# A three-block network on one core: the quarter boundaries and the tail of block 3 in another order

## The chip, the core and the metric

The kernel runs on one core of one Trainium2 chip. TensorE (PE) multiplies, VectorE (DVE), ScalarE (ACT) and GpSimd (POOL) do the rest, and SyncE (SP) issues most transfers; each engine runs its own list of instructions in order and waits on semaphores. The metric is the time of one whole execution on the device, in microseconds, as the median of several runs.

## What is computed

Three blocks follow each other on 2048 rows of 1024 float32 numbers; the change is in the third. Its reference, cut to what matters:

```python
h = einsum('btd,de->bte', x, w_in) + b_in            # 36 column tiles of 128
q_a, k_a, v_a, g_a, q_h, z_fwd, z_bwd, i_h, g_h = split(h, ...)
o_a = neighbourhood_attention(q_a, k_a, v_a, rpb) * silu(g_a)
logf_f, k_f = hgrn2_forget(z_fwd, ...)
logf_b, k_b = hgrn2_forget(z_bwd, ...)
o_fwd = hgrn2_chunk_scan(q_h, k_f, i_h, logf_f)      # S_t = f_t S_{t-1} + k_t v_t
o_bwd = flip(hgrn2_chunk_scan(flip(q_h), flip(k_b), flip(i_h), flip(logf_b)))
o_h = o_fwd + o_bwd
o_h = o_h * rsqrt(mean(square(o_h), -1) + RMS_EPS) * hg_norm_gain * silu(g_h)
y = einsum('bte,ed->btd', concatenate([o_a, o_h], -1), w_out) + b_out
r = DEEPNORM_ALPHA * x + y
out = (r - mean(r)) * rsqrt(var(r) + LN_EPS) * ln_gain + ln_bias
```

## The kernel before, in words

Every float32 factor of the large products is split into a high part and the remainder, and each product is three matmuls (high x high, high x low, low x high).

**Quarters.** Block 3 works on four quarters of 512 rows. In each, 36 column tiles of the input projection run (24 matmuls of 512 columns each, L3804 to L3806, or the same work by rows, L3814 to L3816). Between them stand pieces of attention and of the recurrence. At the start of a quarter x is needed transposed and split: `turn_x` i is, for row tile i of 16, eight transposes into two PSUM banks (x2_turn, L3045), a copy by ScalarE that makes the high part (x2_high, L3055), and a subtraction by VectorE for the low part (x2_low, L3062). Two SBUF buffers hold row tiles, so tile i + 2 can be loaded only after tile i is transposed, and the two PSUM banks are shared with the projection.

**Recurrence.** 64 units (quarter, head, direction, half). For each, `el` is 15 VectorE and 11 ScalarE instructions that make the scaled factors, `prod` (products, L3823 to L3845) sums small blocks into one PSUM bank, opened and closed by matmuls of zeros (L3823, L3834), `state` and `out` (outputs, closed by L3877) follow one and two slots later. The backward direction has no running state yet: its states come last, in 16 chain units n = 0 to 15, four heads of the last quarter first.

**Tail.** Chain unit n loads four 128x512 pieces (`ch_ld`: query, key-value, output so far, gate), VectorE makes four states (chain_state, L3748, L3751), TensorE multiplies them with the query (L3948), VectorE adds (`ch_o`, L3686), ScalarE squares (`sq`), TensorE sums over channels (`fin`, L3957), ScalarE makes the root as logarithm and exponential (`fin_root`, L3450, L3453), VectorE scales and gates (`fin2`, L3691, L3693), and SyncE stores the result to y_tiles in HBM (L3273). The output projection takes 16 row tiles from the last row to the first. Each loads its y tile (`y_ld`, L3296), splits it (`y_split`: ACT L3458, DVE L3701), and multiplies it in two halves of 24 matmuls of 512 columns (`o`, L254 to L256) with w_out, which was loaded (`wo`, L3251), and split by ScalarE (L3438) and GpSimd (L3781, `wo_split`). x is loaded (`x_ld`), GpSimd adds the bias to it (L3787), which VectorE has scaled once (`o_scale`, L3696), VectorE adds the product (`o_sum`, L3707), takes statistics of both halves (`o_end`, L3713), and normalises (L3718, L3724) with a root from ScalarE (`o_root`, L3463, L3465).

**Order.** One list, L.order, made by b3_order, holds all these steps; each engine walks through it and emits its part of each step. A step is placed before or behind a slot (`before`, `after`); slots 0 to 143 are the projection tiles, 36 to a quarter, slots behind that the tail. Inside a slot a rank decides.

## Time and profile before

| | us |
|---|---|
| median of 3 runs (lowest, highest) | 4450.73 (4446.66, 4456.67) |
| the profiled execution | 4447.12 |
| its span | 4445.2 |

Stretches of the span (us from its start), TensorE's busy time in them, its granted clock as a share of 2.4 GHz, and the busy share of the 16 DMA engines:

| stretch | what runs | PE busy | clock | DMA |
|---|---|---|---|---|
| 2900 to 3080 | most of quarter 0 | 151.1 of 180 | 0.85 to 1.00 | 0.71 to 0.86 |
| 3120 to 3160 | first boundary | 23.4 of 40 | 0.85, 0.72 | 0.91, 0.47 |
| 3160 to 3180 | quarter 1 | 20.0 of 20 | 1.00 | 0.45 |
| 3440 to 3480 | second boundary | 31.0 of 40 | 1.00, 0.74 | 0.62, 0.39 |
| 3760 to 3800 | third boundary | 31.0 of 40 | 1.00, 0.74 | 0.58, 0.42 |
| 4160 to 4240 | end of the recurrence, chain units | 33.9 of 80 | 0.59 to 0.74 | 0.44 to 1.01 |
| 4260 to 4320 | chain units and out projection | 60.0 of 60 | 1.00 | 0.33 to 0.68 |

How to read it: busy time of TensorE is no measure of speed, since its matmuls overlap; its idle time is what a better order can win. A wait has a releaser, the last event it waited for, and a wait that ends costs only if nothing else ends later.

### The profile page before, as it was taken

How to read it: one execution, taken by the hardware profiler on the slowest of the kernel's cores; microseconds unless marked ns; L12 is line 12 of the kernel's file. 1: busy time of each engine (PE TensorE's matmuls, PEld its weight loads, DVE VectorE, ACT ScalarE, POOL GpSimd, SP SyncE). 2: the span in 40 equal slices, each digit the busy share in tenths (PEclk: the TensorE clock that was granted, in tenths of full speed). 3: DMA queues.
4: the chain of work that ended last, by engine and by line, in shares of the span. 5: the costliest groups of instructions: out<-in, count | busy, mean ns of one | idle time of the engine just before them, and what ended most of it. 6: DMA issues, size and time to landing. Idle time of an engine off the chain costs nothing.

```text
span 4445.2 us, 62175 instructions
## 1 busy us (share of the span) xinstructions
PE 4200.8 (95%) x24346; PEld 3427.1 (77%) x24346; DVE 2689.6 (61%) x4238; ACT 1799.4 (40%) x3434; POOL 664.2 (15%) x308
## 2 busy tenths in 40 slices
PE   6999999999999999999999989988899999999689
PEld 5888888889888877788777768867787787777467
DVE  6788888872666643045377767555456546466466
ACT  5111111111566631122466556445445446355553
POOL 2111111110333321111012212322000000000111
PEclk9999999999999999999999999999999999999799
DMA  5111111122544431111488872578666466556553
GB/s 184 43 53 53 52 53 53 53 72 93 192 128 128 124 116 48 64 58 73 174 265 294 271 273 105 192 226 282 218 208 199 159 209 197 182 182 199 187 184 131
DMA packets 515499, 663.94 MB, mean 149 GB/s; under 512 B 60476, under 2 KB 407424, under 8 KB 491786
## 3 DMA queue, kind: packets, MB, share of 16 engines
q1 hardware_dynamic: 466778, 577.13, 40.0%
q10 hardware_dynamic: 48432, 82.85, 5.0%
q8 instruction: 195, 3.19, 0.3%
q14 instruction: 94, 0.77, 0.1%
HBM read 442.24 MB, written 217.65 MB: 148 GB/s over the span
## 4 chain that ended last, share of the span: by engine, by line
PE 78%; DMA 6%; DVE 6%; ACT 4%; SPq 3%; issue 2%; POOL 1%; ACTq 0%; DVEq 0%; POOLq 0%
PE ps L229 11%; PE ps L230 11%; PE ps L231 11%; PE ps L255 3%; PE ps L254 3%; PE ps L256 3%; PE ps L3804 3%; DMA w_split_tiles<-w 3%; PE ps L3805 3%; PE ps L3806 3%; PE ps L3924 2%; PE ps L242 1%; PE ps L243 1%; PE ps L244 1%; PE ps L3893 1%
## 5 line engine op out<-in xcount | busy, mean ns | idle before, releaser
L229 PE MATMUL ps<-hh,wsplit 128*128 128x512 f32 x2048 | 819.9, 400 | 5.5 <-DVE hl L953 3.7
L230 PE MATMUL ps<-hl,wsplit 128*128 128x512 f32 x2048 | 808.6, 395 | 0.0
L231 PE MATMUL ps<-hh,wsplit 128*128 128x512 f32 x2048 | 807.8, 394 | 0.0
L982 DVE SCALAR_TENSOR_TENSOR conv_acc<-conv_in,pcol,conv_acc 128x1024 f32<-128x1024 f32 x480 | 687.4, 1432 | 14.8
L229 PEld LDWEIGHTS ps<-hh,wsplit 128*128 128x128 f32 x2048 | 386.5, 189 | 98.2 <-issue 7.8
L230 PEld LDWEIGHTS ps<-hl,wsplit 128*128 128x128 f32 x2048 | 390.1, 190 | 91.6 <-issue 4.3
L231 PEld LDWEIGHTS ps<-hh,wsplit 128*128 128x128 f32 x2048 | 388.6, 190 | 88.9
L221 POOL TENSOR_TENSOR wsplit<-wraw,wsplit 128x1024 fp32r<-128x1024 f32 x72 | 203.8, 2841 | 1327.6 <-ACT wsplit L216 1327.6
L3804 PE MATMUL ps<-h_hi,w 128*128 128x512 f32 x896 | 377.5, 421 | 18.5 <-DVE b_ost L3527 6.1
L3805 PE MATMUL ps<-h_lo,w 128*128 128x512 f32 x896 | 356.9, 398 | 0.0
L3806 PE MATMUL ps<-h_hi,w 128*128 128x512 f32 x896 | 355.9, 397 | 0.0
L733 ACT ACTIVATE b_sig<-ps 128x512 f32<-128x512 f32 x64 | 38.3, 600 | 502.5 <-PE ps L231 502.0
L3804 PEld LDWEIGHTS ps<-h_hi,w 128*128 128x128 f32 x896 | 171.4, 191 | 62.8 <-DVE b_ost L3527 6.7
L3805 PEld LDWEIGHTS ps<-h_lo,w 128*128 128x128 f32 x896 | 172.8, 193 | 41.0 <-issue 0.3
L3806 PEld LDWEIGHTS ps<-h_hi,w 128*128 128x128 f32 x896 | 171.8, 192 | 39.7
L254 PE MATMUL ps<-wo,o_yh 128*128 128x512 f32 x448 | 177.4, 396 | 3.1 <-DVE o_yl L1108 3.1
L3781 POOL TENSOR_TENSOR wo<-wo_raw,wo 128x1024 fp32r<-128x1024 f32 x8 | 18.5, 2344 | 1076.2 <-ACT wo L3438 1076.2
L256 PE MATMUL ps<-wo,o_yl 128*128 128x512 f32 x448 | 176.6, 394 | 0.0
L255 PE MATMUL ps<-wo,o_yh 128*128 128x512 f32 x448 | 176.5, 394 | 0.0
L3814 PE MATMUL ps<-w,h_hi 128*128 128x256 f32 x512 | 153.9, 301 | 12.0 <-POOL w L3018 10.0
L242 PE MATMUL ps<-wsplit,hh 128*128 128x256 f32 x512 | 147.6, 288 | 5.0 <-POOL wsplit L221 5.0
L3815 PE MATMUL ps<-w,h_hi 128*128 128x256 f32 x512 | 148.3, 290 | 0.0
(427 smaller groups left out, 8765.0 us busy)
## 6 DMA issues: line engine op xcount, KB each, us to landing
w<-w_split_tiles SPq DMA_DIRECT2D x108, 1024.0 KB, 5.4
wraw<-in_w_in SPq DMA_DIRECT2D x72, 512.0 KB, 3.9
w_split_tiles<-w SPq DMA_DIRECT2D x36, 1024.0 KB, 6.9
sh<-hy_ak ACTq DMA_DIRECT2D x48, 512.0 KB, 4.0
g_tiles<-b_ost SPq DMA_DIRECT2D x80, 256.0 KB, 5.6
w_raw<-in_w_in SPq DMA_DIRECT2D x36, 512.0 KB, 4.7
wo_raw<-in_w_out SPq DMA_DIRECT2D x32, 512.0 KB, 6.3
sh<-hy_ad ACTq DMA_DIRECT2D x32, 512.0 KB, 8.7
```

Of the source, the lines that this page charges most:

```text
L221: e.tensor_tensor(self.H[:, n % self.ring, 1024:2048], self.raw[:, n % 2, :], self.H[:, n % self.ring, 0:1024], ALU.subtract).then_inc(*c. ...
L229: e.matmul(p[:, :], wh, c.HH[tb][:, k, :], start=k == 0, stop=False)
L230: e.matmul(p[:, :], wh, c.HL[tb][:, k, :], start=False, stop=False)
L231: t = e.matmul(p[:, :], wl, c.HH[tb][:, k, :], start=False, stop=k == 7)
L242: e.matmul(out, hh, wh, start=k == 0, stop=False)
L254: e.matmul(p[:, :], yh(k), wh, start=k == 0, stop=False)
L255: e.matmul(p[:, :], yh(k), wl, start=False, stop=False)
L256: t = e.matmul(p[:, :], yl(k), wh, start=False, stop=k == KT - 1)
L982: e.scalar_tensor_tensor(v, a[:, h * 1024 + j:(h + 1) * 1024 + j], c.convw(j, ch), v, ALU.mult, ALU.add) \
L3804: e.matmul(p[:, :], wh, L.HH[:, k, :], start=k == 0, stop=False)
L3805: e.matmul(p[:, :], wh, L.HL[:, k, :], start=False, stop=False)
L3806: t = e.matmul(p[:, :], wl, L.HH[:, k, :], start=False, stop=k == 7)
```

## The change

**Boundaries.** The first two row tiles of a quarter are loaded four slots sooner. `turn_x` i, i + 1, i + 2 and i + 3 no longer come in two pairs, but with the steps of the slot between them, and all four ahead of the element step `el`. The load of tile i + 2 is issued by ScalarE behind its copy of tile i, not by SyncE.

**Zeros.** L3834 and L3877 are gone; the last real matmul closes the sum.

**Tail.** w_out tiles 0 to 3 and chain unit 0 are loaded within the last slots of the projection. Units 1 to 4, the attention half of y tile 0, w_out 4 to 7, and units 5 to 9 follow behind the recurrence, then the three constants. The first four units' root and scaling are done in one group, and fin2 writes the 128 columns of row tile 15 straight into the buffer of y tile 0. The out projection begins in slot 158 instead of 160. Its statistics are taken per half behind each sum, and its root is now an addition and a reciprocal by VectorE and one square root by ScalarE.

```diff
-    L.cb, L.fb = Banks(c, c.P[5:6]), Banks(c, c.P[6:8])
+    L.cb, L.fb = Banks(c, c.P[5:6]), Banks(c, c.P[6:8] + c.P[2:4])
...
     for k in range(8):
-        after(148 if k < 4 else 150, "wo", k)
+        after((143, 144, 141, 142)[k] if k < 4 else c0 + 1, "wo", k)
     for k in range(0, 8, 4):
-        after(151 if k < 4 else 153, "wo_split", k)
-    c0 = 149
+        after(c0 if k < 4 else c0 + 7, "wo_split", k)
     for n in range(16):
         s = c0 + n
-        after(c0 if n < 4 else c0 + 4 if n < 10 else c0 + 8 if n < 12 else c0 + 11 if n < 14 else c0 + 13, "ch_ld", n)
+        after(c0 - 5 if n < 1 else c0 if n < 5 else c0 + 2 if n < 10 else c0 + 9 if n < 12 else c0 + 11 if n < 14 else c0 + 13, "ch_ld", n)
         after(s + 1, "chain", n)
         after(s + 2, "ch_o", n)
         after(s + 3, "sq", n)
         after(s + 3, "fin", n)
-        if n % 2:
-            after(s + 4, "fin_root", n)
-            after(s + 5, "fin2", n)
-    o0 = c0 + 11
-    after(c0 + 1, "o_const")
-    after(o0 - 4, "o_scale")
+        if n == 3:
+            after(s + 3, "fin_root", 0, 1, 2, 3)
+            after(s + 3, "fin2", 0, 1, 2, 3)
+        elif n % 2 and n > 3:
+            after(s + 4, "fin_root", n - 1, n)
+            after(s + 5, "fin2", n - 1, n)
+    o0 = c0 + 9
+    after(c0 + 5, "o_const")
+    after(o0 - 1, "o_scale")
     for i in range(16):
         s = o0 + 2 * i
-        after(s - 2, "y_ld", i)
+        after(s - 2 if i else c0 + 1, "y_ld", i)
...
-        if s in L.begin and s:
-            L.order += [("turn_x", 4 * (s // 36) + j) for j in range(2, 4)]
         if s < 144:
             L.order += slots[s]
-            if s + 6 in L.begin:
-                L.order += [("row_ld", 4 * ((s + 6) // 36) + j) for j in range(2)]
+            if s + 10 in L.begin:
+                L.order += [("row_ld", 4 * ((s + 10) // 36) + j) for j in range(2)]
             L.order += [("put", u) for u in (slots[s - 1] if s else [])]
         if s == 144:
             L.order += [("put", u) for u in slots[143]]
+        late = sorted(post.get(s, []), key=lambda x: 30 if x[0] == "el" else rank.get(x[0], 20))
         if s + 1 in L.begin:
-            L.order += [("turn_x", 4 * ((s + 1) // 36) + j) for j in range(2)]
-        L.order += sorted(post.get(s, []), key=lambda x: 30 if x[0] == "el" else rank.get(x[0], 20))
+            i = 4 * ((s + 1) // 36)
+            early = [x for x in late if x[0] in ("ld", "w_st", "out", "state")]
+            mid = [x for x in late if x not in early and x[0] != "el"]
+            L.order += [("turn_x", i)] + early + [("turn_x", i + 1)] + mid + [("turn_x", i + 2), ("turn_x", i + 3)] + [x for x in late if x[0] == "el"]
+        else:
+            L.order += late
...
-        elif k == "turn_x" and s[1] >= 4 and s[1] % 4 < 2:
-            row_ld(s[1] + 2)
...
-            if s[1] == 0:
+            k = s[1]
+            if k < 4:
+                for n in range(140, 144):
+                    if w3_slot(n) == k:
+                        e.wait_ge(*L.done[L.last_unit[n]])
+                    if n % 4 == k:
+                        e.wait_ge(*L.w_ld[k][n])
+            else:
                 e.wait_ge(*L.done[L.last_unit[143]])
-            if s[1] >= 4:
-                e.wait_ge(*L.wo_hi[s[1] - 4])
+                e.wait_ge(*L.wo_hi[k - 4])
...
+            if n < 4:
+                e.wait_ge(*L.o_st[n % 2][12 + n])
             if n == 0:
+                for u in (first_of(3, 0) + 2, first_of(3, 0) + 3):
+                    e.wait_ge(*L.qe_st[u % 4][u])
+                    e.wait_ge(*L.kv_st[u % 2][u])
+                stored((3, "rg", 0))
+            elif n == 1:
                 e.wait_ge(*L.r_pe[63, "out", 1])
-                for q in L.qe_st + L.kv_st + L.o_st + L.ost_st:
+                for q in L.qe_st + L.kv_st + L.ost_st:
...
+                m = 384 if n < 4 else 512
                 e.wait_ge(*L.fin_d[n, 1])
                 if n >= 4:
                     e.wait_ge(*L.ry_st[n % 4][n - 4])
-                e.dma_start(c.Y[4 + hd][:, 512 * tb:512 * tb + 512], L.CB[chain_buffer(n)][:, 2, :]).then_inc(*L.ry_st[n % 4].up(n))
+                e.dma_start(c.Y[4 + hd][:, 512 * tb:512 * tb + m], L.CB[chain_buffer(n)][:, 2, 0:m]).then_inc(*L.ry_st[n % 4].up(n))
...
+            if i == 0:
+                for w in att_needed(L, it):
+                    e.wait_ge(*L.y_st[w % 2][w])
+                e.dma_start(L.Y2raw[b][:, 1024:1536].rearrange("p (k t) -> p k t", k=4), c.Y[0:4, :, it * 128:(it + 1) * 128].rearrange("k p t -> p k t")) \
+                    .then_inc(*L.y_ld[b].up(i))
+                continue
...
+            elif i:
+                e.wait_ge(*L.ry_st[3][3])
...
             x2_high(e, c, i)
+            if i % 4 < 2:
+                e.wait_ge(*L.tr[i, 1])
+                x2_load(e, c, i + 2)
...
-            e.wait_ge(*L.o_dve["mv", i])
-            e.activation(v, L.sto[:, i % 2, 13:14], ACT.Ln, bias=L.eps5).then_inc(*L.o_act.up((i, 0)))
-            e.wait_ge(*L.o_act[i, 0])
-            e.activation(v, v, ACT.Exp, scale=-0.5).then_inc(*L.o_act.up((i, 1)))
+            e.wait_ge(*L.o_dve["inv", i])
+            e.activation(v, v, ACT.Sqrt).then_inc(*L.o_act.up((i, 1)))
...
+                if n < 4:
+                    to = L.Y2raw[0][:, 1536 + 128 * hd:1664 + 128 * hd]
+                    e.tensor_tensor(to, yo[:, 384:512], ga[:, 384:512], ALU.mult).then_inc(*L.fin_d.up((n, "y")))
+                e.tensor_tensor(yo[:, 0:m], yo[:, 0:m], ga[:, 0:m], ALU.mult).then_inc(*L.fin_d.up((n, 1)))
...
+            e.wait_ge(*c.by_dve["out", 3, i, h])
+            e.bn_stats(L.sto[:, i % 2, 6 * h:6 * h + 6], X[:, sl]).then_inc(*L.o_dve.up(("st", i, h)))
         elif k == "o_end":
             i = s[1]
             X, st = L.XO[:, i % 3, :], L.sto[:, i % 2, :]
-            e.wait_ge(*c.by_dve["out", 3, i, 1])
-            for h in range(2):
-                e.bn_stats(st[:, 6 * h:6 * h + 6], X[:, h * 512:(h + 1) * 512]).then_inc(*L.o_dve.up(("st", i, h)))
             e.wait_ge(*L.o_dve["st", i, 1])
             e.bn_aggr(st[:, 12:14], st[:, 0:12]).then_inc(*L.o_dve.up(("mv", i)))
             e.wait_ge(*L.o_dve["mv", i])
+            e.tensor_scalar(st[:, 14:15], st[:, 13:14], 1e-5, None, ALU.add).then_inc(*L.o_dve.up(("var", i)))
+            e.wait_ge(*L.o_dve["var", i])
+            e.reciprocal(st[:, 14:15], st[:, 14:15]).then_inc(*L.o_dve.up(("inv", i)))
...
-                e.matmul(p[k0:k0 + m, q0:q0 + h], lhs, x[:, bl, qs], start=False, stop=False)
-        e.matmul(p, c.zb[:, 0:128], c.zb[:, 0:256], start=False, stop=True)
+                e.matmul(p[k0:k0 + m, q0:q0 + h], lhs, x[:, bl, qs], start=False, stop=lv == 2 and bl >= 4)
...
-            t = e.matmul(p[:, ps], L.VH[:, 2 * h + j, hd * 128:(hd + 1) * 128], L.AT[:, n % 2, js], start=False, stop=False)
-            if d == 1 and h == 1 and j == 1:
-                t = e.matmul(p[:, :], c.zb[:, 0:128], c.zb[:, :], start=False, stop=True)
+            t = e.matmul(p[:, ps], L.VH[:, 2 * h + j, hd * 128:(hd + 1) * 128], L.AT[:, n % 2, js], start=False, stop=d == 1 and h == 1 and j == 1)
```

What this does to the engines' lists, at the places the prediction speaks of. In after.py lines stand further down: L3045 is L3052 there, L3062 is L3069, L3266 is L3284, L3251 is L3262, L3781 is L3818, L3787 is L3824.

TensorE at the second boundary (last matmul of slot 71, then the transposes of tiles 8 and 9), before and now:

```order
L3806 MATMUL ps<-h_hi,w_211 128x512
L3045 MATMUL ps<-ident,x_rows_sb 128x128 x16
L3855 MATMUL ps<-rec_v,rec_kdt 128x128 x2
L3893 MATMUL ps<-att_pt,att_v 64x64 x6
L3931 MATMUL ps<-ident,att_e 128x128 x3
```

```order
L3843 MATMUL ps<-h_hi,w_211 128x512
L3052 MATMUL ps<-ident,x_rows_sb 128x128 x8
L3891 MATMUL ps<-rec_v,rec_kdt 128x128 x2
L3052 MATMUL ps<-ident,x_rows_sb 128x128 x8
L3927 MATMUL ps<-att_pt,att_v 64x64 x6
L3965 MATMUL ps<-ident,att_e 128x128 x3
```

The state product (L3855, now L3891) has moved between the transposes of tiles 8 and 9.

VectorE at the same place; L3570 to L3579 (now L3589 to L3610) are the element step, L3062 (now L3069) x4 are the low parts of tiles 10 and 11:

```order
L3570 TENSOR_TENSOR rec_k_1_243<-rec_k_1_243,rec_k 128x8x16
L3572 TENSOR_TENSOR rec_x_237<-rec_x_237,rec_q 128x8x16
L3574 TENSOR_TENSOR rec_kd<-rec_kd,rec_k 128x256
L3575 TENSOR_TENSOR rec_qd<-rec_qd,rec_q 128x256
L3577 TENSOR_TENSOR rec_ke<-rec_ke,rec_k 128x256
L3579 TENSOR_TENSOR rec_qe<-rec_qe,rec_q 128x256
L3062 TENSOR_TENSOR h_lo<-ps,h_hi 128x4x128 x4
L3505 TENSOR_SCALAR rec_f<-rec_f,lower_bound 128x512
L3509 TENSOR_SCALAR rec_k<-rec_f 128x512
```

```order
L3666 COPY_PREDICATED rec_at<-pair,ps 128x256
L3671 COPY rec_kdt<-ps 128x256
L3069 TENSOR_TENSOR h_lo<-ps,h_hi 128x4x128 x4
L3694 RECIPROCAL att_st<-att_st 128x1
L3696 TENSOR_SCALAR att_e<-att_e,att_st 128x384
L3589 TENSOR_TENSOR rec_x_235<-rec_w,rec_b 128x256
L3589 TENSOR_TENSOR rec_x_236<-rec_w,rec_b 128x256
L3589 TENSOR_TENSOR rec_x_237<-rec_w,rec_b 128x256
L3591 TENSOR_TENSOR rec_qd<-rec_w,rec_b 128x256
```

The low parts stood behind the whole element step and now stand ahead of it, behind the copies of `prod`.

SyncE behind the last slots, from the w_out loads on; chain_buf_252 is the buffer of unit 0, 253 of unit 1:

```order
L3251 DMA wo_raw<-in_w_out 128x1024 x4
L3245 DMA rec_o_rows<-rec_o 128x512
L3266 DMA chain_buf_252<-chain_q_rows 128x512
L3266 DMA chain_buf_252<-chain_kv_rows 128x512
L3266 DMA chain_buf_252<-rec_o_rows 128x512
L3266 DMA chain_buf_252<-g_tiles 128x512
L3266 DMA chain_buf_253<-chain_q_rows 128x512
L3266 DMA chain_buf_253<-chain_kv_rows 128x512
L3266 DMA chain_buf_253<-rec_o_rows 128x512
L3266 DMA chain_buf_253<-g_tiles 128x512
L3266 DMA chain_buf_254<-chain_q_rows 128x512
L3266 DMA chain_buf_254<-chain_kv_rows 128x512
```

```order
L3262 DMA wo_raw<-in_w_out 128x1024
L3284 DMA chain_buf_252<-chain_q_rows 128x512
L3284 DMA chain_buf_252<-chain_kv_rows 128x512
L3284 DMA chain_buf_252<-rec_o_rows 128x512
L3284 DMA chain_buf_252<-g_tiles 128x512
L3240 DMA chain_q_rows<-rec_qe 128x256 x2
L3235 DMA y_tiles<-att_y 128x256
L3245 DMA chain_kv_rows<-rec_kvs 128x256 x2
L3250 DMA rec_o_rows<-rec_o 128x512
L3284 DMA chain_buf_253<-chain_q_rows 128x512
L3284 DMA chain_buf_253<-chain_kv_rows 128x512
L3284 DMA chain_buf_253<-rec_o_rows 128x512
```

Unit 0 is loaded ahead of the recurrence's last stores, and unit 1 directly behind the last of them; four w_out loads have left this place.

GpSimd, its last instructions; w_211 are block 3's input weights, wo the output weights, o_x the rows of x:

```order
L3773 MEMSET rec_k_1_243 128x512
L3018 TENSOR_TENSOR w_211<-w_raw,w_211 128x1024 x32
L3781 TENSOR_TENSOR wo_215<-wo_raw,wo_215 128x1024 x8
L3787 TENSOR_TENSOR o_x<-o_x,o_bias 128x1024 x16
L4027 UNCONDITIONAL_BRANCH
```

```order
L3025 TENSOR_TENSOR w_211<-w_raw,w_211 128x1024 x32
L3818 TENSOR_TENSOR wo_215<-wo_raw,wo_215 128x1024 x4
L3824 TENSOR_TENSOR o_x<-o_x,o_bias 128x1024
L3818 TENSOR_TENSOR wo_215<-wo_raw,wo_215 128x1024 x4
L3824 TENSOR_TENSOR o_x<-o_x,o_bias 128x1024 x15
L4063 UNCONDITIONAL_BRANCH
```

The low parts of w_out 4 to 7 stood ahead of all x tiles and now stand behind the first one, which waits for the scaled bias (`o_scale`).

## Rows read from the trace of the kernel before

**Rows 1.** Windows: us, busy us (count) of PE, PEld, DVE, ACT, POOL; clock, DMA, GB/s.
```profile
3120.00:3140.00 20.00, 12.20 (x83) 9.38 (x82) 13.71 (x43) 12.31 (x34) 0.00 (x0) 0.85 0.91 330
...
4200.00:4220.00 20.00, 9.73 (x38) 6.53 (x38) 10.65 (x25) 14.19 (x19) 8.13 (x4) 0.74 1.01 378
...
4260.00:4280.00 20.00, 20.00 (x95) 16.09 (x94) 18.52 (x31) 15.58 (x21) 2.41 (x1) 1.00 0.68 210
```

**Rows 2.** Timeline of TensorE, first boundary: start, us, instruction, [idle before and releaser].
```profile
3146.80 1.94 PE L3045 MATMUL ps<-ident,x_rows_sb 128*128 128x128 f32 x8 [11.21 <-DMA x_rows_sb<-x_rows]
...
3152.73 0.47 PE L3804 MATMUL ps<-h_hi,w 128*128 128x512 f32 x1 [1.46 <-DVE h_lo L3062]
```

**Rows 3.** Timeline, first boundary: ScalarE's last copy of tile 4.
```profile
3129.11 0.60 ACT L3055 ACTIVATE h_hi<-ps 128x512 fp32r<-128x512 f32 x1 [0.26 <-PE ps L3045]
```

**Rows 4.** Timeline of the SyncE queue, first boundary: row tiles 6 and 7.
```profile
3141.65 0.93 SPq L3036 DMA_DIRECT2D x_rows_sb<-x_rows  x2
```

**Rows 5.** All row tile loads by line L3036, issue to landing.
```profile
DMA to landing us min/median/max: 3.1/6.6/9.0
```

**Rows 6.** Timeline of all engines, second boundary.
```profile
3458.53 0.42 DVE L3640 COPY rec_kdt<-ps 128x256 f32<-128x256 f32 x1
...
3463.61 1.28 DVE L3062 TENSOR_TENSOR h_lo<-ps,h_hi 128x512 fp32r<-128x512 f32 x2
3464.36 1.97 PE L3045 MATMUL ps<-ident,x_rows_sb 128*128 128x128 f32 x8 [5.80 <-DVE h_lo L3062]
...
3467.79 0.77 PE L3804 MATMUL ps<-h_hi,w 128*128 128x512 f32 x1 [1.46 <-DVE h_lo L3062]
```

**Rows 7.** Timeline of TensorE, a closing zero matmul and what follows it.
```profile
3118.81 0.28 PE L3834 MATMUL ps<-zeros 128*128 128x256 bf16 x1
3118.93 0.61 PE L3839 MATMUL ps<-rec_qd,rec_kd 128*128 128x128 f32 x4
```

**Rows 8.** Timeline of all engines, from the recurrence's end.
```profile
4168.50 0.38 PE L3877 MATMUL ps<-zeros 128*128 128x512 bf16 x1
...
4173.99 9.26 POOL L3781 TENSOR_TENSOR wo<-wo_raw,wo 128x1024 fp32r<-128x1024 f32 x4 [1060.55 <-ACT wo L3438]
...
4178.11 0.33 SPq L3266 DMA_DIRECT2D chain_buf<-chain_q_rows  x1
...
4185.49 0.23 DVE L3748 COPY rec_s<-chain_buf 128x128 f32<-128x128 f32 x1 [18.76 <-DMA chain_buf<-g_tiles]
```

**Rows 9.** Timeline of all engines, chain units up to the first out projection.
```profile
4208.22 1.51 DVE L3751 SCALAR_TENSOR_TENSOR rec_s<-rec_s,chain_dec,chain_buf 128x128 f32<-128x128 f32 x4 [9.46 <-DMA chain_buf<-g_tiles]
...
4212.40 0.75 DVE L3691 SCALAR_TENSOR_TENSOR chain_buf<-chain_buf,pcol,fin_n 128x512 f32<-128x512 f32 x1
...
4213.18 0.69 DVE L3693 TENSOR_TENSOR chain_buf<-chain_buf 128x512 f32<-128x512 f32 x1
...
4227.94 2.34 POOL L3787 TENSOR_TENSOR o_x<-o_x,o_bias 128x1024 f32<-128x1024 f32 x1 [19.82 <-DMA o_x<-x_rows]
...
4238.20 1.23 DVE L3701 TENSOR_TENSOR o_y<-o_y_raw,o_y 128x1024 fp32r<-128x1024 f32 x1 [10.62 <-ACT o_y L3458]
...
4244.59 0.77 PE L254 MATMUL ps<-wo,o_y 128*128 128x512 f32 x1
```

**Rows 10.** DMA issues from 4160 to 4260: count, size, us to landing.
```profile
o_shift<-in_ln_bias SPq DMA_DIRECT2D x1, 512.0 KB, 14.2
```

**Rows 11.** The chain that ended last, in order of time, first half's end and the end.
```profile
4251.46 0.86 PE ps L3957 x2
4252.32 0.89 PE ps L3948 x8
...
4436.72 0.70 DVE o_x L3707
4437.44 1.30 DVE o_st L3713 x2
...
4439.32 1.28 ACT L3465
```

23 lines of the change are left out of this document (15 added, 8 removed).

## The prediction

> **What bounds the kernel now.** I read the page first: TensorE is busy for 4200.8 of 4445.2 us, so only two things can make this kernel faster, fewer TensorE instructions or less TensorE waiting. Then the table by windows, to find where TensorE waits inside block 3, and there the timelines of all engines. Three kinds of place stand out. At the three quarter boundaries TensorE waits for new rows of x: at the first one 11.21 us for a row transfer [rows 2], at the second 5.80 us for VectorE [rows 6]; the third repeats the second, with the same 5.80 us. Between the last recurrence matmul at 4168.50 and the first out-projection matmul at 4244.59 [rows 8, 9] lie 76 us, most of which TensorE spends waiting (9.73 us busy of 20 in the middle of it [rows 1]). And behind the last out-projection matmul there is a serial end of about 9 us [rows 11]. All of these are what the diff touches. Elsewhere in block 3 TensorE is the bound, with one exception: quarter 0, where the ring of weight tiles waits for its own stores and TensorE idles about a sixth of the time (the table by stretches above).
>
> **Closing zero matmuls.** 64 units lose one of 256 columns, 16 blocks lose one of 512. The profiler gives the small one 0.28 us, but matmuls overlap: the next one starts 0.12 us later [rows 7]. That is the price on the path, and twice that for 512 columns. 64 x 0.12 + 16 x 0.24 = 11.5 us if TensorE is the bound everywhere. In quarter 0 (a quarter of them) weights are the bound, and in the last 40 us of the recurrence it is latency; there I count almost nothing. I take 8.5 us, ends 5 and 11.5. Nothing is reordered by it.
>
> **First boundary.** The SyncE queue issued row tiles 6 and 7 at 3141.65 [rows 4], because it sat behind loads of attention values; TensorE was ready for them at 3135.6 and had them at 3146.80. From there to the first projection matmul of quarter 1 it took 5.9 us more [rows 2]. Now ScalarE issues each of these loads itself, right behind its copy of the tile two before, which ended at 3129.71 [rows 3]. A row load took 3.1 to 9.0 us to land, median 6.6 [rows 5]: tile 6 is there at 3136.3, tile 7, issued 2.4 us later, at 3138.7, when the banks for it are free as well. So the projection starts at about 3136.3 + 5.9 = 3142.2 instead of 3152.73: 10.5 us. With 9.0 us to land, tile 7 comes at 3141.1 and the gain is 8; with the shortest, TensorE's own work until 3135.6 is the limit and it is 11.2. I take 10. Two more instructions on ScalarE's queue cost it some half a microsecond each; it had 0.6 us to spare between its copies.
> The Trainium skill (Trainium Kernel Development and Optimization, Key Constraints) says that all issuing queues share the same 16 DMA engines, so that another issuer saves issue time alone. In this window these engines were 91% busy [rows 1], so the rule points to the long landing: 8 us for this place instead of 10.
>
> **Second and third boundary.** Row tiles are in time there. TensorE waits because VectorE first makes a whole recurrence element step and only then the low part of tile 10: it was free at 3458.95 (3458.53 + 0.42) and made the low part at 3463.61 [rows 6]. The new order puts this step behind tiles 10 and 11. That frees the bank 4.7 us sooner, and the chain behind it (3.4 us from 3464.36 to 3467.79) moves as it is. The element step itself comes later on VectorE, but its product is wanted three projection slots (over 15 us) later, and VectorE idled behind this step before: covered. Moving tile 9 behind the state product costs nothing, since TensorE had a gap for its bank. Over this wait the granted clock falls to the lower of its two levels, 1.2 instead of 2.4 GHz (0.74 on average from 3460 to 3480), and the first matmuls behind it run at half speed for some 4 us; a shorter gap may give back up to 1.9 us. I take 5 for each, 10 for both, ends 8 and 14.
>
> **Earlier row loads.** The first two tiles of a quarter are loaded four slots sooner. Where they stood, nobody waited for them. For quarters 2 and 3 this is free. In quarter 0 they now enter a stretch in which weights are late, and 1 MB ahead of a weight tile takes 2.8 us of issue: I count 1 us lost, ends 0 and 3.
>
> **Start of the tail.** Before, the SyncE queue first issued four w_out tiles, then stored the recurrence's last output behind them, waited for it, and began the chain loads at 4178.11; VectorE had its first unit at 4185.49 [rows 8]. Now w_out tiles 0 to 3 and chain unit 0 are loaded during the recurrence, and units 1 to 4 go out at about 4170.6, 7.5 us sooner. Unit 0 starts at once, but what sets the start of the out projection is further back. I follow it through the new order, with durations of [rows 8, 9, 11]:
> (a) Chain unit 5 is loaded behind units 1 to 4 and w_out 4 to 7. Before, unit 4 stood in that place and also behind three constants, and came at 4208.22 [rows 9]. Minus 7.5, minus 1.5 MB of constants at the 378 GB/s of this stretch [rows 1] (4.0), minus 1.7 because less then waits in the queues, gives 4195, ends 4191 and 4199.
> (b) fin of unit 3 stands behind chain unit 5 on TensorE, and ScalarE makes all four roots in one group: about 4 us to the end of the last logarithm, a table load of 1.28 and the first exponential, 0.6: 4201.
> (c) fin2 for four units: 0.75 + 0.69 as before, cut in two pieces, some 0.1 more each: 6.2 us, to 4207.4.
> (d) VectorE then adds unit 5's output (0.69), does chain unit 6 (1.51), output 6 (0.69), chain 7 (1.51), the split of y tile 0 (1.23) and scales the bias (0.69), with handoffs 7 us: 4214.4. The y tile is no limit: its upper half is made in place.
> (e) On GpSimd the first x tile, which waits for that bias, now stands ahead of the low parts of w_out 4 to 7. So 2.34 us for x, and then four low parts in 9.26 us: 4226.3. **This is the last wait to end.** The first half's matmuls with k = 4 to 7 come one by one behind them, so this half ends at about 4227; before, it ended at 4251.46 [rows 11].
> That is 24.3 us sooner. Against it: the half now stands behind chain unit 8, not 10, so two chain units (0.89 each) and two fins (0.86) more follow it [rows 11]: 3.5 us. A first half with waits in it will leave the clock at its lower level a little longer: 1.5 us. Net 19.3, ends 11 and 27.
> VectorE is close to the bound while chain units and out projection run together: 18.52 of 20 us [rows 1]. The fullest slot gets one statistics instruction more (0.65): the statistics of half 0 move into the slot that also has a y split, a normalisation and two fin2. I add 0.65 + 0.65 (sum and statistics) + 1.23 + 1.28 + 2.9, then 1.0 until the next chain state: 7.7 us. TensorE needs 5.6 + 0.86 twice over the border, 8.2 us. It fits, with 0.5 us to spare where there was 1.1.
>
> **The very end.** The chain was sum 0.70, two statistics 1.30, aggregate, logarithm, table load 1.28, exponential, normalisation [rows 11]. Now one of the statistics is already made, and ScalarE has a single square root with no table load left near it, beside VectorE's 1.28 us centring. Against 2 x 0.65 and 1.9 us of ScalarE stand 0.65 and two small VectorE instructions: 1.0 us, ends 0.5 and 2.
> The Trainium skill (ScalarE: Activation LUTs, Table sets: the hidden batching unit) has logarithm and exponential in one set, so that the pair needs one load, and says that a square root after an exponential needs one. By it the new form would add loads while fins run and save none at the end, 0.4 us gained rather than 1.0. The trace speaks against it: a load of 1.28 us stands before the exponentials too [rows 11].
>
> **Sum.** 8.5 + 10 + 10 - 1 + 19.3 + 1.0 = 47.8 us. From the profiled run's 4447.12 us (span 4445.2 and 1.9 around it) that makes 4399.3; the median of the runs is 3.6 us above that run, so in the medians it is 4450.73 - 47.8, about **4403 us**.
>
> **The rivals.**
> 1. The transfers are the bound of the tail. In (a) everything hangs on one unit behind 6 MB; the constants stand behind 20 chain loads, and in the trace one of them took 14.2 us to land [rows 10]. If unit 5 or the constants come 8 us later than I think, the out projection starts 8 us later: 4411. For it: the DMA engines are full there, 1.01 [rows 1]. Against: the volumes ahead are counted.
> 2. VectorE becomes the bound of the mixed part. Five full slots that overshoot by 1 to 2 us each: about 4411. For it: the margin of 0.5 us; against: it has held so far at 8.3 us of work in that slot, since the other slot is light.
> 3. Everything comes at the good ends: unit 5 at 4191, the clock kept at the boundaries, all zeros worth their 0.12. About 4391.
> 4. The boundary gains are given back. If the weight ring or the attention loads of the SyncE queue set the pace behind a boundary, TensorE waits a little later instead. That costs 20 us: 4423. Against it: after each boundary TensorE was busy throughout, and the SyncE queue waited for TensorE to free a weight tile, not the other way.
> 5. Slower than before. The one mechanism that could do it is (e): the low parts of w_out hang on GpSimd behind a constant that is loaded last. The half ends 13 us after the bias is scaled; to cancel all the rest it must end at 4275, so the constants must land after 4262, some 67 us after issue, against 14.2 measured [rows 10].
>
> **How the numbers follow.** Forecast 0.60, rival 1 0.14, rival 2 0.09, rival 3 0.11, rival 4 0.04, rival 5 0.01, and 0.01 for no change. Forecast's own range is 4396 to 4410, from the ends of the terms taken together; rivals 1, 2 and 3 lie mostly within 4389 to 4418, which leaves out rival 4 and the far ends of rivals 1 and 3. 0.2% (9 us) is about what a measurement of this kernel can tell from no change. Even rival 4 is 28 us faster, so faster gets 0.97, same 0.02, slower 0.01.
>
> **What would show it.** TensorE's wait for row tiles at the first boundary is under 2 us, and the 5.80 us for VectorE at the other two are gone. The first out-projection matmul starts about 48 us behind the last recurrence matmul, and its half ends 58 us behind it; before, these were 76 and 83 us. In that half TensorE waits for GpSimd's low parts, and GpSimd for the bias. Wrong would be: a wait of TensorE for transfers in the mixed part, VectorE waits in front of chain units, or a first half that starts over 70 us behind the recurrence.

## The result, and the profile after

| | before, us | after, us |
|---|---|---|
| median of 6 runs each (lowest, highest) | 4452.92 (4446.66, 4456.67) | 4426.20 (4420.79, 4431.92) |
| the profiled execution | 4447.12 | 4420.79 |
| its span | 4445.2 | 4419.0 |

The ratio of after to before is 0.9938, 95% interval 0.9928 to 0.9949: the change makes the kernel 26.7 us faster. The prediction said 4403, range 4389 to 4418: a gain of 47.8 us, 21 us more than came. The direction was right, the size was not.

Blocks 1 and 2 are the same in all kernels, and yet block 3's first transposes start between 2817.8 and 2828.1 us in the profiled runs shown here. So, beside medians, I compare **block 3's own time**, from these transposes to the end of the span: 1626.6 us before, 1597.6 after. That is 29.0 us less; the other 2.8 us of the difference between 26.2 (the spans) and 29.0 come from a later start of block 3 in the profile of after. Cut at the first transposes of row tiles 4, 8 and 12, at the first projection matmul behind each, and at ScalarE's copy of the recurrence's last output (4168.91 before, 4153.34 after), it is:

| stretch of block 3 | before | after | gain | predicted |
|---|---|---|---|---|
| quarter 0 | 306.6 | 308.6 | -2.0 | |
| first boundary | 27.5 | 16.8 | +10.7 | +10 |
| quarter 1 | 296.8 | 297.2 | -0.3 | |
| second boundary | 18.3 | 16.7 | +1.6 | +5 |
| quarter 2 | 302.3 | 300.8 | +1.5 | |
| third boundary | 18.3 | 15.9 | +2.3 | +5 |
| quarter 3 with the recurrence's end | 380.6 | 376.1 | +4.6 | |
| quarters together (zeros, row loads) | | | +3.7 | +7.5 |
| recurrence end to the end of the first half | 82.6 | 64.9 | +17.7 | +24.3 |
| from there to the last sum | 185.2 | 193.2 | -7.9 | -5 |
| from the last sum to the end | 8.5 | 7.6 | +0.9 | +1 |

**First boundary**, TensorE's timeline. Against [rows 2] (11.21 us for tile 6), tile 6 costs 2.17 us and tile 7 3.56; the start of the projection behind them is 16.8 us behind the first transposes instead of 27.5. The first row below stands inside the transposes of tile 4, where TensorE waits for ScalarE's copy of the last projection tile; before, this wait was 2.62 us (at 3128.41):

```profile
3131.31 0.66 PE L3052 MATMUL ps<-ident,x_rows_sb 128*128 128x128 f32 x4 [0.75 <-ACT b_ost L3383]
...
3138.57 1.22 PE L3052 MATMUL ps<-ident,x_rows_sb 128*128 128x128 f32 x8 [2.17 <-DMA x_rows_sb<-x_rows]
3143.36 1.94 PE L3052 MATMUL ps<-ident,x_rows_sb 128*128 128x128 f32 x8 [3.56 <-DMA x_rows_sb<-x_rows]
3146.76 0.77 PE L3841 MATMUL ps<-h_hi,w 128*128 128x512 f32 x1 [1.46 <-DVE h_lo L3069]
```

**Second boundary**, TensorE, and then ScalarE's and SyncE's DMA issues (ACTq and SPq). The wait of 5.80 us for VectorE [rows 6] is gone, and in its place stand 2.70 and 0.92 us for row tiles, which were in time before:

```profile
3454.30 1.94 PE L3052 MATMUL ps<-ident,x_rows_sb 128*128 128x128 f32 x8 [2.70 <-DMA x_rows_sb<-x_rows]
3457.16 1.94 PE L3052 MATMUL ps<-ident,x_rows_sb 128*128 128x128 f32 x8 [0.92 <-DMA x_rows_sb<-x_rows]
3460.56 0.77 PE L3841 MATMUL ps<-h_hi,w 128*128 128x512 f32 x1 [1.46 <-DVE h_lo L3069]
```

```profile
3444.11 0.32 SPq L3003 DMA_DIRECT2D w<-w_split_tiles  x1
...
3445.49 1.53 SPq L3162 DMA_DIRECT2D att_q<-g_tiles  x2
...
3446.23 0.33 ACTq L3043 DMA_DIRECT2D x_rows_sb<-x_rows  x1
...
3448.30 0.33 ACTq L3043 DMA_DIRECT2D x_rows_sb<-x_rows  x1
...
3449.90 1.77 SPq L3136 DMA_DIRECT2D g_tiles<-b_ost  x1
```

While ScalarE issues the two row tiles (3446.23, 3448.30), SyncE sends a weight tile, the attention's inputs and a store, from 3444.11 on. The transposes of tile 10 begin at 3454.30, 8.1 us behind its issue. In between, the 16 transfer engines are 97% busy and move 350 GB/s (window as in [rows 1]):

```profile
3446.20:3454.20 8.00, 5.09 (x64) 3.53 (x63) 4.95 (x10) 4.54 (x8) 0.00 (x0) 0.95 0.97 350
```

**Start of the tail.** VectorE and then GpSimd between the arrival of chain unit 5 and the end of the first half, to be read beside [rows 9]:

```profile
4183.77 1.52 DVE L3788 SCALAR_TENSOR_TENSOR rec_s<-rec_s,chain_dec,chain_buf 128x128 f32<-128x128 f32 x4 [6.33 <-DMA chain_buf<-g_tiles]
4190.18 0.75 DVE L3723 SCALAR_TENSOR_TENSOR chain_buf<-chain_buf,pcol,fin_n 128x512 f32<-128x512 f32 x1 [4.89 <-ACT fin_n L3483]
...
4203.23 9.23 DVE L3788 SCALAR_TENSOR_TENSOR rec_s<-rec_s,chain_dec,chain_buf 128x128 f32<-128x128 f32 x4
4212.39 0.68 DVE L3717 TENSOR_TENSOR chain_buf<-chain_buf,ps 128x512 f32<-128x512 f32 x1
4212.99 5.05 DVE L3788 SCALAR_TENSOR_TENSOR rec_s<-rec_s,chain_dec,chain_buf 128x128 f32<-128x128 f32 x4
4218.24 0.69 DVE L3742 SCALAR_TENSOR_TENSOR o_x<-o_x,ps 128x512 f32<-128x512 f32 x1 [0.20 <-PE ps L256]
```

```profile
4202.87 2.35 POOL L3824 TENSOR_TENSOR o_x<-o_x,o_bias 128x1024 f32<-128x1024 f32 x1 [38.65 <-DVE o_bias L3731]
4205.18 9.53 POOL L3818 TENSOR_TENSOR wo<-wo_raw,wo 128x1024 fp32r<-128x1024 f32 x4
```

Four states of a chain unit (L3788) take 1.51 us [rows 9, L3751]. At 4203.23 they take 9.23 us and at 4212.99 5.05 us, in both cases beside GpSimd's subtractions and additions; the sum at 4212.39, whose second input is in PSUM, keeps its 0.68. TensorE starts the first half at 4210.60, behind unit 8's last two matmuls, which waited for the third of the slow states that begin at 4203.23. The clock is granted at 0.77 on average from 4210 to 4220:

```profile
4210.15 0.80 PE L3982 MATMUL ps<-chain_buf,rec_s 128*128 128x128 f32 x2 [1.56 <-DVE rec_s L3788]
4210.60 0.77 PE L254 MATMUL ps<-wo,o_y 128*128 128x512 f32 x1
```

**Mixed part.** The chain that ended last (start, duration, and what held the chain) runs three times over the same steps:

```profile
4268.72 0.70 DVE chain_buf L3728
4269.81 4.90 DMA o_x<-x_rows
4274.78 2.39 POOL o_x L3824
4278.61 1.21 DVE o_y L3736
```

That is: VectorE gates a chain output (L3728), SyncE stores it, and only then, in its queue, issues the load of the next x tile (4269.81), to which GpSimd adds the bias (4274.78). VectorE waits for that.

### The profile page after: what moved, and what is told of

Its sections match the earlier page's. It is cut to its first block and busy times, and to the rows that moved or that the text cites. A ratio compares the mean times of both kernels' runs of the same rounds, so it can differ in the third digit from the quotient of the medians.

```text
span 4419.0 us, 61999 instructions
## 1 busy us (share of the span) xinstructions
PE 4198.2 (95%) x24266; PEld 3425.1 (78%) x24266; DVE 2706.3 (61%) x4274; ACT 1755.8 (40%) x3389; POOL 664.5 (15%) x308
## 5 line engine op out<-in xcount | busy, mean ns | idle before, releaser
L3818 POOL TENSOR_TENSOR wo<-wo_raw,wo 128x1024 fp32r<-128x1024 f32 x8 | 18.8, 2379 | 1038.7 <-ACT wo L3468 1038.7
```

## Experiments

All line numbers in rows are those of the kernel named. Each kernel's ratio is to the kernel before on the same chip. There were several chips, and the kernel before took 4454.5 to 4457.7 us on them, so ratios compare versions better than medians do. Stretches are those of one profiled execution of each kernel. How far they scatter can be seen where nothing was changed: the first boundary takes 15.3 to 18.5 us in the kernels that have the changed kernel's order, loads by ScalarE and early rows there; the first half ends 64.8 to 65.0 us behind the recurrence in four kernels with the changed kernel's order up to there.

### Zeros alone

```diff
-                e.matmul(p[k0:k0 + m, q0:q0 + h], lhs, x[:, bl, qs], start=False, stop=False)
-        e.matmul(p, c.zb[:, 0:128], c.zb[:, 0:256], start=False, stop=True)
+                e.matmul(p[k0:k0 + m, q0:q0 + h], lhs, x[:, bl, qs], start=False, stop=lv == 2 and bl >= 4)
...
-            if d == 1 and h == 1 and j == 1:
-                t = e.matmul(p[:, :], c.zb[:, 0:128], c.zb[:, :], start=False, stop=True)
```

> The kernel before with the closing matmuls of zeros left out, nothing else. The prediction priced them at 8.5 us (64 x 0.12 and 16 x 0.24 with quarter 0 and the end counted at almost nothing). Theory A, from the two traces: these matmuls lie on the path only where nothing else is late; the four quarters together gained some 3.7 us besides the boundaries, so this run is 3 to 5 us faster than before (about 4448.5). Theory B, the prediction's: the whole 8.5 us come here, and the earlier row loads then cost 5 us elsewhere; 4444. The quarters' stretches between the boundaries show which: each of quarters 1 and 2 shorter by 1 to 1.5 us (A) or by 2.5 us (B).

Measured: ratio 0.9998 (0.9989 to 1.0007), so between 4.9 us faster and 3.1 slower; theory B's 8.5 us are excluded, A's 3 to 5 are not shown either. The quarters take 306.7, 297.4, 301.7 and 377.1 us: quarter 1 not shorter, quarter 2 by 0.6, quarter 3 by 3.5. But the third boundary takes 19.8 us instead of 18.3 and the tail 0.9 us more, and block 3's own time is 1625.4 us, only 1.2 less than before. Why the small zeros are worth next to nothing can be seen in one unit. TensorE and its weight loads (PEld) in the kernel before, and then in this one:

```profile
3169.29 0.29 PE L3833 MATMUL ps<-rec_x,rec_k 128*32 128x16 f32 x12
3169.51 0.28 PE L3834 MATMUL ps<-zeros 128*128 128x256 bf16 x1
3169.63 0.61 PE L3839 MATMUL ps<-rec_qd,rec_kd 128*128 128x128 f32 x4
3170.07 0.38 PE L3845 MATMUL ps<-ident,rec_ke 128*128 128x128 f32 x2
```

```profile
3169.51 0.54 PEld L3839 LDWEIGHTS ps<-rec_qd,rec_kd 128*128 128x128 f32 x4
```

```profile
3171.82 0.29 PE L3833 MATMUL ps<-rec_x,rec_k 128*32 128x16 f32 x12
3172.04 0.71 PE L3838 MATMUL ps<-rec_qd,rec_kd 128*128 128x128 f32 x4
3172.59 0.38 PE L3844 MATMUL ps<-ident,rec_ke 128*128 128x128 f32 x2
```

```profile
3172.04 0.52 PEld L3838 LDWEIGHTS ps<-rec_qd,rec_kd 128*128 128x128 f32 x4
```

From the last group of small products to the transposes behind (L3845, L3844) it is 0.78 us with the zero matmul (3169.29 to 3170.07) and 0.77 without (3171.82 to 3172.59). The weights of the next matmuls load from 0.22 us on in both (3169.51, 3172.04); before, the zero matmul ran under this load, and without it TensorE waits for the load. Over all 64 units, counted from the last small product alone, the median is 0.68 us with the zero matmul and 0.66 without. The large zero is worth more: from the four output matmuls (L3875) to the next step 0.75 us with it (3192.49 to 3193.24) and 0.54 without (3195.00 to 3195.54, its L3874). So the price is 64 x 0.01 to 0.02 and 16 x 0.21, 4 to 5 us and not 11.5, and less where TensorE is not the bound. That makes some 1.0 us a quarter; why quarter 3 gained 3.5 and quarter 1 nothing stays open, and the scatter of a quarter is about 1 us.

### Zeros and boundaries, tail as before

The kernel above with the boundary part of the change (its order, ScalarE's loads, the earlier first rows), word for word as in the diff ahead: the lines on `row_ld`, `turn_x`, `late`, `x2_high` and `row3_ld`.

> The kernel before with the zeros left out and the quarter boundaries of the changed kernel (order of the turn steps, the loads of tiles i + 2 issued by ScalarE, the first two row tiles four slots earlier); the tail is that of before. It splits the gain: what is missing to the changed kernel is the tail's. Theory A, by the boundaries as the two traces show them: zeros 3.7, first boundary 10.7, second 1.6, third 2.3, together 18.3 us faster than before: about 4434.5. Theory B, the prediction's sizes: 8.5 + 10 + 10 - 1 = 27.5 us: about 4425, as fast as the whole changed kernel; it would mean that the new tail brings nothing.

Measured: 4438.7 against 4454.5, ratio 0.9964 (0.9950 to 0.9977), 16 us; block 3's own time 1610.5, 16.1 less than before. That is near A and far from B. The boundaries take 16.8, 16.4 and 15.9 us, as in the changed kernel. The tail of the changed kernel therefore brings the rest, 12.9 us of block 3's own time; against the tail of the kernel before it is 10.7, since the same old tail took 2.1 us longer in this execution (278.4 and 276.3).

### Row loads by SyncE again

```diff
         elif k == "turn_x":
             i = s[1]
             x2_high(e, c, i)
-            if i % 4 < 2:
-                e.wait_ge(*L.tr[i, 1])
-                x2_load(e, c, i + 2)
```

and in SyncE's list `elif k == "turn_x" and s[1] % 4 < 2: row_ld(s[1] + 2)`.

> The changed kernel with the loads of row tiles i + 2 issued by SyncE again, at the place of the turn step in the list, instead of by ScalarE; the order of the steps stays. Theory A: at the second and third boundary the new waits for row tiles (2.70 + 0.92 and 1.90 + 1.00 us) are there because SyncE, which no longer waits for the transposes in front of a row load, sends a weight tile, the attention loads and a store at that moment, which share the transfer engines with the two row tiles (they took 6 to 8 us to land, 3.1 to 3.7 when SyncE sent them ahead of everything). With SyncE issuing them these boundaries take 13 to 14 us instead of 16.65 and 15.93, and the first one 16.8 to 20 (the row tiles stand in SyncE's queue again, though ahead of the attention loads); in all 3 to 6 us faster than the changed kernel. Theory B: the transfers take as long whoever issues them (the first boundary shows 6 to 8 us too), the waits stay at 2 to 3 us, and the time is within 1 us of the changed kernel, 4426.

Measured: 4423.65, ratio 0.9935 (0.9923 to 0.9948); block 3's own time 1597.3, the same. But its parts moved: first boundary 25.2 us (16.8), second 12.35 (16.65), third 12.72 (15.93). TensorE at the first and at the second boundary:

```profile
3151.25 1.94 PE L3051 MATMUL ps<-ident,x_rows_sb 128*128 128x128 f32 x8 [11.46 <-DMA x_rows_sb<-x_rows]
```

```profile
3464.24 1.04 PE L3051 MATMUL ps<-ident,x_rows_sb 128*128 128x128 f32 x8
3466.35 1.24 PE L3051 MATMUL ps<-ident,x_rows_sb 128*128 128x128 f32 x8 [1.08 <-DVE h_lo L3068]
3469.05 0.47 PE L3839 MATMUL ps<-h_hi,w 128*128 128x512 f32 x1 [1.46 <-DVE h_lo L3068]
```

Theory A holds for the second and third boundary: the wait for rows is gone there, and with it 7.5 us (A's 3 to 6 us in the whole did not come, because the first boundary gives 8.4 back). SyncE's two tiles landed 3.3 and 5.1 us behind their issue, ScalarE's first one 7.9. That ScalarE's queue is slow by itself is unlikely: in an earlier block of the changed kernel its stores of 512 KB landed in a median 2.6 us. That SyncE's transfers take the engines away fits this and the 97% above, but no run holds these transfers back and leaves ScalarE's loads in place. Against the kernel before the two boundaries gain 5.9 and 5.5, where the prediction had 5 each. At the first boundary A's bound of 20 us was too low: tile 6 waits 11.46 us, as before the change [rows 2], because SyncE's queue gets to it late. Who issues decides, at each place the other way round.

### GpSimd's low parts one slot earlier

```diff
-        after(c0 if k < 4 else c0 + 7, "wo_split", k)
+        after(c0 if k < 4 else c0 + 6, "wo_split", k)
```

> The changed kernel with the split of w_out tiles 4 to 7 one slot earlier: ScalarE makes their high parts behind the square of unit 3 and ahead of the four logarithms, in its gap from 4178 to 4187, and GpSimd the low parts right behind, ahead of the first x tile, while VectorE waits for chain unit 5. Theory A (GpSimd blocks VectorE): the chain states of units 8 and 9, which took 9.23 and 5.05 us beside GpSimd's subtractions, are back at 1.5 us or at most at 1.5 plus the rest of one x addition (2.4); TensorE gets unit 8 some 7 us sooner, the first out-projection matmul starts 50 to 52 us behind the end of the recurrence instead of 57.6, and the run is 5 to 8 us faster than the changed kernel: 4419 to 4421. Theory B (the slow chain states have another cause, transfers or the clock): they stay at 5 to 9 us, and the time is within 2 us of 4426.

Measured: 4427.4, ratio 0.9942 (0.9930 to 0.9955): no gain, the first half ends 65.9 us behind the recurrence (64.9). GpSimd and VectorE:

```profile
4185.09 9.31 POOL L3818 TENSOR_TENSOR wo<-wo_raw,wo 128x1024 fp32r<-128x1024 f32 x4 [14.44 <-ACT wo L3468]
```

```profile
4190.58 4.74 DVE L3788 SCALAR_TENSOR_TENSOR rec_s<-rec_s,chain_dec,chain_buf 128x128 f32<-128x128 f32 x4 [6.37 <-DMA chain_buf<-g_tiles]
...
4213.29 5.27 DVE L3788 SCALAR_TENSOR_TENSOR rec_s<-rec_s,chain_dec,chain_buf 128x128 f32<-128x128 f32 x4
```

Theory A's mechanism is there: the states of unit 8 took 5.27 instead of 9.23 us, beside two x additions of 4.71 together, and unit 9's are back at 1.51. But its gain is not: the low parts now held up unit 5's states (4190.58, 4.74 us), which stand ahead of the closing of the first four units. The blocking moved with the work.

### The low parts doubled

Each of the four subtractions is preceded by one of the same operands and size. It writes into the buffer of x tile 2; so SyncE, not shown, holds that tile's load, and what stands behind it in its queue, until the last subtraction is done. This bears on the time, not on the states below.

```diff
             for q in range(s[1], s[1] + 4):
                 e.wait_ge(*L.wo_hi[q])
+                if q >= 4:
+                    e.wait_ge(*L.ry_st[3][3])
+                    e.tensor_tensor(L.XO[:, 2, :], L.WOraw[:, q, 1024:2048], L.WO[:, q, 0:1024], ALU.subtract)
```

> The changed kernel with each of GpSimd's four subtractions for w_out tiles 4 to 7 preceded by another one of the same operands and size that writes to an unused buffer (so that the work of GpSimd at this place is doubled, 19 us instead of 9.5). Theory A: GpSimd's instructions hold VectorE's two-input SBUF instructions off. The states of units 8 and 9 stretch on: together from 14.3 us to 22 or more, unit by unit with GpSimd's instruction ends; VectorE instructions that read PSUM or one SBUF input keep their 0.68. The first half ends 8 to 10 us later, and the run takes 4434 to 4437. Theory B: only TensorE waits for the low parts, and the chain states keep their 9.2 and 5.1 us; the half ends 9 us later all the same, so the length of the chain states tells the theories apart, not the time.

Measured: 4437.15, ratio 0.9949 (0.9934 to 0.9964); the half ends 8.1 us later (+ 73.0). VectorE and GpSimd:

```profile
4212.95 9.29 DVE L3790 SCALAR_TENSOR_TENSOR rec_s<-rec_s,chain_dec,chain_buf 128x128 f32<-128x128 f32 x4
4222.16 0.68 DVE L3719 TENSOR_TENSOR chain_buf<-chain_buf,ps 128x512 f32<-128x512 f32 x1
4222.76 9.14 DVE L3790 SCALAR_TENSOR_TENSOR rec_s<-rec_s,chain_dec,chain_buf 128x128 f32<-128x128 f32 x4
```

```profile
4214.88 2.41 POOL L3822 TENSOR_TENSOR o_x<-wo_raw,wo 128x1024 f32<-128x1024 f32 x1
4217.38 2.34 POOL L3824 TENSOR_TENSOR wo<-wo_raw,wo 128x1024 fp32r<-128x1024 f32 x1
4219.68 2.42 POOL L3822 TENSOR_TENSOR o_x<-wo_raw,wo 128x1024 f32<-128x1024 f32 x1
```

Eight states took 18.4 us instead of 14.3 and of 3.0 undisturbed, each about as long as one GpSimd instruction (2.3 to 2.4); A's 22 was too high, since there are only eight states and each waits for one instruction. The sum from PSUM between them keeps 0.68. This is A: GpSimd's two-input instruction holds off a VectorE instruction that reads both inputs from SBUF, for as long as it runs. It is not limited to two inputs: at 4162.67 in the changed kernel a copy of one 128x128 piece took 1.64 us instead of 0.22, until GpSimd's low part beside it ended.

### The low parts on VectorE

The same four subtractions are emitted by VectorE, ahead of chain unit 5, and their high parts by ScalarE ahead of the logarithms. GpSimd keeps tiles 0 to 3.

```diff
+        elif k == "wo_dve":
+            for q in range(4, 8):
+                e.wait_ge(*L.wo_hi[q])
+                e.tensor_tensor(L.WO[:, q, 1024:2048], L.WOraw[:, q, 1024:2048], L.WO[:, q, 0:1024], ALU.subtract).then_inc(*c.by_dve.up(("wo3", q)))
```

> The changed kernel with the low parts of w_out tiles 4 to 7 made by VectorE ahead of chain unit 5 instead of by GpSimd, and their high parts by ScalarE ahead of the logarithms. If GpSimd's two-input subtractions in SBUF block VectorE's two-input instructions (theory A), nothing blocks it now but the x additions: four low parts of about 1.2 us each lie in VectorE's wait of 6.33 us for unit 5, unit 5's states take 1.5 us (4.74 when the low parts were on GpSimd at this place), unit 8's states at most 1.5 plus two x additions, and the first half of the out projection ends 58 to 61 us behind the recurrence's last output instead of 64.9: 4 to 7 us faster than the changed kernel, 4419 to 4422. Theory B (it is the transfers, not GpSimd, that made those states slow): the chain states stay slow wherever transfers are dense, and the time stays at 4426.

Measured: 4423.9, ratio 0.9935 (0.9921 to 0.9948); the tail 263.6 us instead of 265.7. The first half ends at + 62.1 (64.9 in the changed kernel; A's 58 to 61 is just missed). Unit 9's states are back at 1.5 us; unit 8's still take 5.27, beside the two x additions. So moving the low parts off GpSimd gives the first half 2.8 us, with VectorE's own time for them taken off, and the rest of the loss is elsewhere.

### Unit 5 behind the closing of the first four

```diff
+    at = {("chain", 5): 21}
...
-        late = sorted(post.get(s, []), key=lambda x: 30 if x[0] == "el" else rank.get(x[0], 20))
+        late = sorted(post.get(s, []), key=lambda x: at[x] if x in at else 30 if x[0] == "el" else rank.get(x[0], 20))
```

> The changed kernel with chain unit 5 moved behind the closing of the first four units (fin 3, roots, fin2) on all engines; nothing else. Step (a) of the prediction let everything hang on unit 5's data, which stands in front of fin 3 on TensorE though fin 3 does not need it. Theory A: fin2 of the first four units then starts some 9 us sooner (at recurrence end + 27 to 29 instead of + 36.8), but the out projection starts behind chain unit 8 and the bias, which both still hang on transfers: it starts 2 to 5 us sooner, and the run is 2 to 4 us faster than the changed kernel, about 4423. Theory B: unit 5's place sets the start of the whole half, which moves by the full 9 us: about 4417. Theory C: the blocking by GpSimd fills the room, and nothing moves: 4426.

Measured: 4421.3, ratio 0.9924 (0.9912 to 0.9937). fin2 starts at + 27.5 (A: 27 to 29) instead of + 36.8, the first out-projection matmul at + 47.3 instead of + 57.3 (B), but its half ends at + 61.5, only 3.4 us sooner (A). VectorE shows what stands there now:

```profile
4195.00 0.70 DVE L3732 TENSOR_SCALAR o_bias<-o_bias 128x1024 f32<-128x1024 f32 x1 [3.15 <-DMA o_shift<-in_ln_bias]
...
4198.52 9.32 DVE L3789 SCALAR_TENSOR_TENSOR rec_s<-rec_s,chain_dec,chain_buf 128x128 f32<-128x128 f32 x4
```

Unit 5's place did hold the start up. Behind it the bias is scaled only when the last constant has landed (3.15 us of waiting), the low parts follow x on GpSimd as before, and unit 9's states are held off for 9.32 us. TensorE, in the half by then, waits for the low parts four times, 0.8 to 1.4 us each: here they are the last wait, as the prediction's (e) had it.

### What stands ahead of unit 5

Two runs on step (a). In one, the load of y tile 0's attention half moves behind unit 5; in the other SyncE waits for unit 5 to have landed before it issues more:

```diff
+            elif n == 6:
+                e.wait_ge(*L.ch_ld[5][5, "gate"])
```

> The changed kernel with the load of the attention half of y tile 0 (256 KB in pieces of 512 bytes; it took 10.5 us to land) behind chain unit 5 instead of ahead of w_out tiles 4 to 7. Theory A, the small pieces slow the transfers: between 4165 and 4175 they moved 299 to 306 GB/s at a busy share of 1.0, against 386 to 400 later, which makes some 2 us; unit 5 is on VectorE at recurrence end + 28 to + 28.5 instead of + 30.4. Theory B, a shared queue: only its 256 KB count, 0.7 us: + 29.7. If the rate is low for another reason it stays at + 30.4. The whole time moves by as much or less, 4424 to 4426, since GpSimd's blocking of VectorE stands behind it.

> The changed kernel with SyncE waiting for chain unit 5 to have landed before it issues units 6 to 9, the constants and what follows. Theory A: the transfer engines serve what is behind unit 5 together with it; some 1 MB more than stands ahead of unit 5 has moved when it lands (8.75 MB moved from 4155.5 to 4183.8, 7.6 MB issued up to unit 5). Held back, unit 5 is there 2.5 to 3 us sooner, at recurrence end + 27.5. Theory B: transfers of one queue are served in turn, and unit 5 stays at + 30.4. In both, units 6 to 9 and the constants come later, unit 6 no sooner than 7 us behind unit 5, so the whole run is 2 to 8 us slower than the changed kernel: 4428 to 4434.

Measured: with the y tile behind, unit 5 comes at + 29.7 instead of + 30.4, its 256 KB and no more; with units 6 to 9 held back, at + 30.2 (4425.2 and 4429.5 us). B in both: what SyncE has issued is served in turn here, so what stands behind unit 5 does not slow it, and what stands ahead of it costs its own volume, 0.7 us for the y tile, which step (a) had left out. The rest is rate. From the first issue at 4155.46 to unit 5's arrival the 7.6 MB up to it took 28.3 us, 269 GB/s. Before, 8.9 MB up to unit 4 took 30.1 us, 296 GB/s on average. Step (a) took the constants off that time at the 378 GB/s of full flow [rows 1], and 1.7 us more for shorter queues. Three pieces of this stretch in the changed kernel, and then one in the kernel before (columns as in [rows 1]):

```profile
4155.50:4160.00 4.50, 0.00 (x0) 0.00 (x0) 0.17 (x1) 2.74 (x4) 4.50 (x3) 0.61 0.59 127
...
4165.00:4170.00 5.00, 4.22 (x14) 2.59 (x13) 3.00 (x8) 1.26 (x2) 0.00 (x0) 0.50 1.01 299
...
4175.00:4180.00 5.00, 2.90 (x10) 1.41 (x10) 2.10 (x5) 1.45 (x3) 0.00 (x0) 0.70 1.04 400
```

```profile
4193.00:4198.00 5.00, 4.00 (x15) 2.16 (x14) 2.31 (x6) 0.26 (x1) 0.00 (x0) 0.74 1.02 410
```

The first 4.5 us move 127 GB/s, and until 4175 it is 299 to 337 GB/s at a full share; only then 386 to 400. Before, the first 10 us were alike (122 and 356), but then it was 354 in the third piece and 386 to 410 from the fourth on. The changed kernel's 299 and 306 from 4165 to 4175 cost it some 2 us by this comparison. What keeps the rate down in these 10 us is left open; it is 295 and 338 there with the y tile behind unit 5 too, so the small pieces of that tile are not the whole cause.

### x loads ahead of the stores

```diff
-        late = sorted(post.get(s, []), key=lambda x: 30 if x[0] == "el" else rank.get(x[0], 20))
+        late = sorted(post.get(s, []), key=lambda x: 30 if x[0] == "el" else 18 if x[0] == "x_ld" and x[1] > 2 else rank.get(x[0], 20))
```

> The changed kernel with the load of each x tile from tile 3 on placed ahead of the stores of fin2 in SyncE's queue, where it stood right behind them; nothing else. Theory A: the stalls in the mixed part (VectorE waits 4.1, 5.2 and 5.3 us for GpSimd's addition to x, TensorE idle 4.3 us between 4288 and 4318 and at a lower clock behind it) come from x loads that stand behind those stores; they are gone, and the run is 3 to 5 us faster than the changed kernel: about 4422. Theory B: the load then waits for the output store of the tile three before, or TensorE waits for the y tile that comes behind the fin2 stores anyway; the y tile's split is then the wait, and the time stays within 1 us of 4426.

Measured: 4416.8, ratio 0.9922 (0.9908 to 0.9935). From the first half's end to the last sum it takes 188.1 us instead of 193.2, 5.1 less (A). VectorE's waits from 4262 to 4330, of the changed kernel and of this one (engine, line, waited for; sum, times, longest):

```profile
DVE o_x L3742 <- POOL o_x L3824: 14.5, 3, 5.3
```

```profile
DVE o_x L3742 <- PE ps L256: 7.7, 6, 2.3
```

The three waits for GpSimd, 14.5 us, are gone altogether; VectorE now waits for TensorE, as it should.

### First rows late again

```diff
-            if s + 10 in L.begin:
-                L.order += [("row_ld", 4 * ((s + 10) // 36) + j) for j in range(2)]
+            if s + 6 in L.begin:
+                L.order += [("row_ld", 4 * ((s + 6) // 36) + j) for j in range(2)]
```

> The changed kernel with the first two row tiles of a quarter loaded where they were before (six slots ahead, not ten). Theory A: quarter 0, which takes 307.4 to 309.1 us in all kernels with the early loads and 306.6 in the two without, is back at 306.6; boundaries and quarters 1 to 3 stay within 0.5 us: 1.5 us faster, 4424.7. Theory B: the early loads pay at the boundary: without them the first boundary waits for row tiles 4 and 5, 1 to 5 us, and the time is 4427 to 4431. Rival to A: quarter 0's difference is run variation or the removed zeros; it stays at 308.

Measured: 4425.5, ratio 0.9928 (0.9911 to 0.9944). Quarter 0 stays at 309.4, so A is wrong: the earlier loads do not cost the 1 us that the prediction gave them. At the first boundary TensorE waits 3.83 us for ScalarE's copy of the last projection tile, where it was 0.75 with the early loads, and the boundary takes 20.8 us instead of 16.8. In the kernel before, with late rows too, the same wait was 2.62. Row tiles 4 and 5 are not waited for in either, so this is not B's mechanism, though it is B's direction. Why that copy is late then was not followed up. Quarter 0 took 306.6 and 306.7 us in the two kernels with the old boundary and 307.3 to 310.1 in all others, this one too; its cause is open.

### Versions that join what paid

Each is the one before it and one edit more. The first joins three of the edits above, in this order of steps:

```diff
+    at = {("wo_split", 4): 20.1, ("fin2", 0, 1, 2, 3): 20.2, ("chain", 5): 21, ("wo_dve",): 22}
```

> The changed kernel with three edits together: x tiles from tile 3 on loaded ahead of the fin2 stores, chain unit 5 behind the closing of the first four units, and the low parts of w_out tiles 4 to 7 made by VectorE behind chain unit 5 (high parts by ScalarE behind the exponentials). By theory A for each (loads of x behind stores cost 8 us, GpSimd blocks VectorE, unit 5 stood in the way) they add up to 12 to 17 us over the changed kernel: 4409 to 4414. If the starts of the out projection hang on the transfers alone, only the x loads bring something, and it is 4417, as for that edit by itself.

The second lets ScalarE load only tiles 6 and 7, and SyncE the others:

```diff
-            if i % 4 < 2:
+            if i in (4, 5):
                 e.wait_ge(*L.tr[i, 1])
                 x2_load(e, c, i + 2)
...
+        elif k == "turn_x" and s[1] >= 8 and s[1] % 4 < 2:
+            row_ld(s[1] + 2)
```

> The combined version of before (x loads ahead, unit 5 behind, low parts on VectorE) and, in addition, the row tiles i + 2 loaded by ScalarE only at the first boundary and by SyncE at the second and third, as the run with SyncE everywhere showed best for each (first 25.2 us with SyncE against 17.3 with ScalarE; second and third 12.4 and 12.7 against 16.6 and 15.9). Theory A: the boundaries do not touch one another, so the second and third take 12.3 to 12.8 us each and the kernel is 7 us faster than the combined version: about 4406. Theory B: the load order at one boundary shifts the weight ring or the stores, and what is won is lost in the quarter behind (in the run with SyncE everywhere quarter 2 took 299.4 us, not longer): 4413.

The third starts the out projection two slots sooner, with y tile 0 split behind fin2 and the low parts:

```diff
-    o0 = c0 + 9
+    o0 = c0 + 7
```

> The version before with the out projection two slots earlier: y tile 0 is split right behind fin2 of the first four units and the low parts, and its first half stands behind chain unit 6 instead of 8. Theory A: TensorE, which waits most of the time from recurrence end + 29 to + 51, starts the half at + 43 to + 46 instead of + 51.5, and it ends at + 49 to + 52 instead of + 57.3; two chain units and two fins more stand behind it (3.5 us), so the run is 2 to 5 us faster than the version before: 4402. Theory B: VectorE, 88 to 98% busy in the mixed part, becomes its bound with nine chain units in it instead of seven, and the time is the same or up to 4 us longer.

The fourth adds the y tile's load behind unit 5:

> The version with the out projection two slots earlier, with the load of y tile 0's attention half behind chain unit 5. If the small pieces slow the transfers ahead of units 4 and 5, chain unit 4, on which fin 3 waits in TensorE's queue, comes 0.5 to 1.5 us sooner, and unit 5 two: 1 to 2 us faster than without (4404). If they do not, 4405.6 again. It would be slower only if the y tile itself comes late: it is needed at recurrence end + 36.

| kernel | median, us | ratio (95%) | half ends at | then to last sum |
|---|---|---|---|---|
| three edits joined | 4413.4 | 0.9910 (0.9897, 0.9924) | + 57.3 | 188.7 |
| and SyncE's row loads at boundaries 2, 3 | 4407.2 | 0.9882 (0.9867, 0.9896) | + 61.2 | 188.9 |
| and out projection two slots earlier | 4405.6 | 0.9879 (0.9864, 0.9894) | + 50.2 | 195.2 |
| and the y tile behind unit 5 | 4404.9 | 0.9886 (0.9866, 0.9906) | + 52.2 | 194.5 |

The three edits together gave 12.1 us of tail (265.7 to 253.6), more than the 8.2 that they gave one by one (5.0, 1.1 and 2.1). That each had been covered by the next is my reading, not shown by a run of its own. The mixed issue brought both boundaries to 12.4 us and left the quarters behind them as they were (299.4 and 376.6 us, against 300.8 and 376.1 in the changed kernel): theory A. Its half ended 3.9 us later than in the version before it, at the same order of the tail. In both, two of unit 8's states were held off by GpSimd's x additions. In the first version these were the last two, in the second the two ahead of the last, by a difference of 0.5 us between VectorE's place and GpSimd's. TensorE's last matmuls of the unit then came 2.3 us later, and the half behind this longer wait took 7.4 us instead of 5.8, its first eight matmuls 0.43 us apart instead of 0.23; the granted clock was 0.83 on average over the 10 us around it, and 1.00 in the first version. So the place of short VectorE instructions beside GpSimd can still move the end of this half by some 4 us from one version to the next. The earlier out projection does what A says to the half, but 6.3 of its 11.0 us go again behind it, where A had counted 3.5; the last two steps cannot be told from no change by their times. Each of the last three beats both kernels, the changed one by 19 to 21 us in the medians and by 23 to 26 us in the ratios (0.9879 to 0.9886 against 0.9938).

## Why the prediction was wrong, step by step

**Direction and sizes.** The boundaries, the start of the tail and the very end gained, and the mixed part lost, as said. Four groups of terms were off, two of them because a mechanism was overlooked, and they add up to the miss: 3.8 (quarters), 6.1 (second and third boundary), 6.6 (start of the tail) and 2.9 (mixed part), less 0.7 that the first boundary gave more. 47.8 - 18.8 = 29.0, the gain in block 3's own time.

**Closing zeros**: failed by size, 8.5 us against 3.4 in the quarters and 1.2 in block 3's own time of the kernel that has nothing else changed. The step took the distance between two starts [rows 7] as what leaving the first one out would give. It should have asked what the next instruction was doing meanwhile: it was loading weights.

**First boundary**: right in mechanism and size, 10.7 against 10, but the size in part by luck. Tile 6 was there 6.6 us behind its issue and tile 7 9.3, the middle and just over the long end of [rows 5]; the prediction had counted 6.6 for both, so tile 7 was 2.7 late. Against it ScalarE could issue the first of them 2.1 us behind the first transposes (3129.96 to 3132.01), where the prediction had 4.5 from the copy's end in the kernel before (3125.20 to 3129.71), mostly since the wait for ScalarE's copy in front had shrunk from 2.62 to 0.75 us. With loads by SyncE the boundary gains 2.3 us, so 8.4 of the 10.7 are ScalarE's issue. The Trainium skill's rule on shared transfer engines (Trainium Kernel Development and Optimization, Key Constraints) would have given 8 here; its place was the next boundary.

**Second and third boundary**: failed, 3.9 against 10. The step looked at VectorE's order alone and left out that the load of the row tile had been moved to another queue as well: "row tiles are in time there" was true only while SyncE sent them and had nothing else on the way. Freed of the wait in front of them, SyncE sent 1 MB of weights and four attention loads into the same 16 transfer engines. This overlap is what the step had wrong: it put the wait for these rows at nothing, and they were waited for 2.70 and 0.92 us, and 1.90 and 1.00 at the third. The run with SyncE's loads gives 5.9 and 5.5 us against 18.25, so the order alone was sized rightly. The rule quoted at the first boundary was the one to apply here.

**Earlier row loads**: -1 us was not there (the run with the late rows), and a gain of up to 4 us at the first boundary was not foreseen; it hides in the 10.7.

**Start of the tail**: 17.7 against 24.3. Step (a) lost 4.3 us: unit 5 came 30.4 us behind the recurrence, not 26.1. It subtracted 1.7 us for shorter queues that no row showed, left out the y tile (0.7), had the first issue 0.4 us too soon, and met a rate some 2 us worse than before, whose cause is open (4.8 together, the last an estimate from the rates of the windows). (b), (c) and (d) held: 5.9 us for fin2 against 6.2, 6.6 against 7 until the bias is scaled. (e) lost 2.8: x and the low parts took 11.8 us, as predicted (11.6), but VectorE was held off beside them, unit 8's last matmuls came at 4210.15, and the first half began behind them instead of running beside the low parts. So the last wait to end was not the low parts, as (e) has it, and TensorE did not wait for them in that half. Of GpSimd holding off VectorE the prediction said nothing. The Trainium skill (SBUF — State Buffer, Who interferes with whom) states the rule: VectorE and GpSimd share one pair of ports under an exclusive lock, and "A DVE instruction with two SBUF inputs contends with a GpSimd instruction that reads SBUF". The doubled run agrees, with 2.3 to 2.4 us for each state. Before, the low parts of these tiles ran (from 4198.87 on, 9.26 us) while VectorE waited for unit 4 [rows 9], and none of the chain states was slow. But the trace of the kernel before did show the effect elsewhere, and could have warned. In quarter 0 this product of 128x128, which takes 0.28 us a few rows later, stands beside a GpSimd subtraction that runs from 2913.71 for 2.39 us:

```profile
2913.87 2.39 DVE L3570 TENSOR_TENSOR rec_x<-rec_x,rec_k 128x128 f32<-128x128 f32 x1 [2.70 <-ACT rec_x L3366]
```

In the out projection of before, y splits (1.2 us alone) took up to 3.09 us beside the x additions.

**Mixed part**: -7.9 against -5. The two more chain units and fins are as priced: without the stall of the x loads 188.7 us, which is 185.2 + 3.5. The other 5.1 us are the x loads behind fin2's stores, which the prediction did not look at, since the change does not touch them; their place in time it does. Rival 2, VectorE as the bound, was not what happened: its full slot held.

**The very end**: right, 0.9 against 1.0. The Trainium skill (ScalarE: Activation LUTs, Table sets: the hidden batching unit), by which the prediction estimated 0.4, is not borne out: in the changed kernel too ScalarE loads a table for 1.28 us between the last logarithm (4187.52) and the first exponential (4189.52).

**The signs that the prediction named.** The first out-projection matmul came 57.3 us behind the recurrence, not 48, and its half ended at 64.9, not 58; both say that the start of the tail was mis-sized. At the first boundary TensorE waited 2.17 and 3.56 us for rows, not under 2. The 5.80 us for VectorE were gone as said, but the prediction had not asked what would be late next.

**Rivals.** None of them was what happened as a whole. Rival 1 had the right cause for a part, unit 5 late by its transfers, by 4.3 us and not 8. Rival 4, gains given back (4423), comes nearest to the time, but not by its mechanism: the quarters behind the boundaries did not get longer.

## What to carry to other kernels

When a load moves to another queue, ask what the queue that it leaves will send in its place: the wait in front of a load also holds back its neighbours, and that may be what made the load fast. Before moving GpSimd's elementwise work, list the VectorE instructions with two SBUF inputs that will lie beside it, and look in the trace at hand for such a pair that already overlaps. And price a removed matmul by the start of the instruction behind the next one, with and without the weight load that it covered.

## What was not expected of the hardware

A VectorE instruction of 0.35 us took 2.1 to 2.4 us beside a GpSimd one with both inputs in SBUF, while one that read PSUM kept its 0.68 us; a copy of 0.22 us with one input in SBUF was held off too (1.64). A zero matmul of 256 columns was worth 0.01 to 0.02 us of TensorE's time when it was left out, one of 512 columns 0.21. Transfers of one queue were served in turn at the one place where it was tried: holding back the 4.2 MB behind unit 5 moved it by 0.3 us. And with the transfer engines' busy share at 1.0 the rate was 299 to 337 GB/s for 15 us and 386 to 400 after that.
